# Hybrid decoder step on eight cores: the norms' transposes moved from TensorE to DMA transposes on SyncE's queue

## What is computed

```python
xn = rmsnorm(h, ln1)                              # norm 1
q, k, v, u = split(xn @ w_in)                     # 1024 -> 512 | 128 | 128 | 512
q, k = rope(q), rope(k)                           # 16 of 64 dims of each head
a  = band_attention(q, k, v, sink)                # 8 heads, 2 kv heads, window 128, learned sinks
pm = pool_mix(u, windows=(2, 4, 8, 16)) * pool_scale
h  = h + concat(a, pm) @ w_out                    # 1024 -> 1024
xn = rmsnorm(h, ln2)                              # norm 2
h  = h + relu(xn @ w_up)**2 @ w_down              # 1024 -> 4096 -> 1024
```

## Time and profile before

| | |
|---|---|
| median of 3 runs | 2930.97 us (2930.91 to 2939.81) |
| the profiled execution's own time | 2944.05 us |
| its span (slowest core, core 1) | 2942.3 us; all cores 2901.3 to 2942.3 |
| granted TensorE clock, mean | 0.979 to 0.985 of full speed |
| TensorE busy | 2779.2 us, 94% |
| VectorE, ScalarE, GpSimd busy | 1522.4, 1535.3, 195.2 us |
| DMA | 436 MB, 148 GB/s; POOL's queue 42.5%, SyncE's 9.5% of 16 engines |

### The profile page before, as it was taken

The page is one execution under the profiler, slowest core; times in us unless marked ns, Lnnn a source line. Parts: engine busy times, 40 slices in busy tenths (PEclk is TensorE's granted clock), DMA queues, the critical chain, the costliest instruction groups (busy, mean ns, idle before and its releaser), DMA issues.

```text
span 2942.3 us, 52160 instructions; the slowest of 8 cores (2901.3 to 2942.3 us)
## 1 busy us (share of the span) xinstructions
PE 2779.2 (94%) x17074; PEld 1446.1 (49%) x17074; DVE 1522.4 (52%) x3188; ACT 1535.3 (52%) x3835; POOL 195.2 (7%) x336
## 2 busy tenths in 40 slices
PE   4789988979899999999999999999899999999997
PEld 2455434445455555545455555454454545555544
DVE  2444534545355555545555555555455555555543
ACT  3545534545355555545454655555554655555543
POOL 1000100100000000000000000000000000000000
PEclk8999989999999999999999999999999999999999
DMA  9599996664756647353625332443325242342446
GB/s 177 88 145 197 178 243 122 146 169 125 195 137 161 189 113 205 101 195 123 229 87 201 114 142 93 154 132 115 117 99 188 87 167 105 117 158 87 160 145 228
DMA packets 115648, 436.41 MB, mean 148 GB/s; under 512 B 18732, under 2 KB 45324, under 8 KB 80216
## 3 DMA queue, kind: packets, MB, share of 16 engines
q0 software_dynamic: 89024, 335.80, 42.5%
q1 hardware_dynamic: 26360, 97.28, 9.5%
HBM read 442.32 MB, written 79.22 MB: 177 GB/s over the span
## 4 chain that ended last, share of the span: by engine, by line
PE 87%; DMA 9%; ACT 1%; issue 1%; DVE 1%; SPq 0%; POOL 0%; ACTq 0%; DVEq 0%; POOLq 0%
PE ps_all L1165 29%; PE ps_all L1147 29%; PE ps_all L801 10%; PE ps_all L1089 8%; DMA s_wup<-w_up 2%; PE ps_all L587 2%; PE ps_all L952 2%; PE ps_all L994 2%; DMA s_wout<-w_out 2%; DMA h_mid<-s_h 1%; DMA s_wdn<-w_dn 1%; DMA s_h<-x_p 1%; PE ps_all L954 1%; PE ps_all L953 1%; DMA s_kc<-ck 1%
## 5 line engine op out<-in xcount | busy, mean ns | idle before, releaser
L1165 PE MATMUL ps_all<-s_wdn,s_aT 128*128 128x512 bf16 x4288 | 1037.5, 382 | 21.6 <-DMA s_wdn<-w_dn 12.5
L1147 PE MATMUL ps_all<-s_xn2T,s_wup 128*128 128x512 bf16 (+2 forms) x4608 | 1023.8, 367 | 19.5 <-DMA s_wup<-w_up 13.2
L1169 DVE TENSOR_TENSOR s_h<-s_h,ps_all 128x512 f32<-128x512 f32 x1072 | 735.1, 686 | 549.1 <-PE ps_all L1165 524.7
L1147 PEld LDWEIGHTS ps_all<-s_xn2T,s_wup 128*128 128x128 bf16 x4608 | 445.1, 98 | 470.1 <-issue 31.0
L1151 ACT ACTIVATE s_relu<-ps_all 128x512 f32<-128x512 f32 (+2 forms) x576 | 326.0, 566 | 626.1 <-PE ps_all L1147 613.8
L1165 PEld LDWEIGHTS ps_all<-s_wdn,s_aT 128*128 128x128 bf16 x4288 | 406.1, 98 | 450.6 <-issue 36.1
L1152 ACT ACTIVATE s_aT<-s_relu 128x512 bf16<-128x512 f32 (+2 forms) x576 | 346.2, 601 | 39.0 <-PE ps_all L1165 5.4
L801 PE MATMUL ps_all<-s_win,s_xnT 128*128 128x512 bf16 (+1 forms) x1632 | 315.0, 350 | 22.5 <-DMA s_win<-w_in 12.6
L976 ACT ACTIVATE s_P<-ps_all,s_stat 128x256 bf16<-128x256 f32 x520 | 239.2, 476 | 91.4 <-DVE s_stat L966 91.3
L1089 PE MATMUL ps_all<-s_wout,s_mixT 128*128 128x512 bf16 x1072 | 249.8, 384 | 2.0 <-ACT s_mixT L1029 1.9
L801 PEld LDWEIGHTS ps_all<-s_win,s_xnT 128*128 128x128 bf16 x1632 | 160.7, 99 | 176.9 <-issue 36.7
(11 more groups left out here) (130 smaller groups left out, 2016.3 us busy)
## 6 DMA issues: line engine op xcount, KB each, us to landing
s_wup<-up_bf POOLq DMA_DIRECT2D x128, 1024.0 KB, 6.4
s_wdn<-dn_bf POOLq DMA_DIRECT2D x128, 1024.0 KB, 7.2
h_mid<-s_h SPq DMA_DIRECT2D x34, 512.0 KB, 8.1
s_h<-h_mid SPq DMA_DIRECT2D x34, 512.0 KB, 7.9
s_h<-x_p SPq DMA_DIRECT2D x32, 512.0 KB, 9.3
s_wup<-w_up POOLq DMA_DIRECT2D x16, 1024.0 KB, 18.0
s_wdn<-w_dn POOLq DMA_DIRECT2D x16, 1024.0 KB, 19.2
y_p<-s_h SPq DMA_DIRECT2D x32, 512.0 KB, 5.5
```

What stands on the lines that cost most here:

```text
L1147: r = e.matmul(ps_t[bk][:, 0:n], lhsT=wup_t[s][:, k, fc * 128:(fc + 1) * 128], rhs=x2[:, k, 0:n], start=(k == 0), stop=(k == 7))
L1165: r = e.matmul(ps_t[db][:], lhsT=aT[:, fc, j * 128:(j + 1) * 128], rhs=wdn_t[s][:, fc, hf * 512:(hf + 1) * 512], start=(fc == 0), stop=(fc ...
L1169: dve(lambda e, hf=hf, db=db: e.tensor_tensor(out=h_t[hs][:, hf * 512:(hf + 1) * 512], in0=h_t[hs][:, hf * 512:(hf + 1) * 512], in1=ps_t[d ...
```

## The change

From the second group on (`q` > 0), both norms leave TensorE: instead of L587, L592 and L594 one DMA transpose on SyncE's queue reads `xh` and writes `xnT`, or the tile's part of `xn2T`. No PSUM bank is taken for it. Its cost for the planner is 0.1 us of the queue and twice the 256 KB that it reads. The first group keeps its transposes on TensorE, and so do probabilities, attention outputs, q and k, and the cached keys in all groups. Where loads of x and constants waited for the first transposes on TensorE (`first_pe`), they wait for the DMA in its place if it is one.

```diff
+    def dma_T(out, in_, reads, writes, pw=(), sembuf=None):
+        def fn(e):
+            return [e.dma_start_transpose(out=out, in_=in_)]
+        return S.op("sp", fn, reads=reads, writes=writes, pwrites=pw, dma=1, sembuf=sembuf, cost=0.1, nbytes=2 * _nbytes(in_))
...
         dve(lambda e: e.scalar_tensor_tensor(out=xh[:], in0=h_t[hs][:], scalar=sT[:, 2:3], in1=g_t[gi][:], op0=ALU.mult, op1=ALU.mult),
             [h_b[hs], sB, g_b[gi]], [xhb], cost=1.29)
+        if bank is None:
+            t_op = dma_T(dstT, xh[:], [xhb], [dstT_b], sembuf=dstT_b)
+            if gi == 0:
+                first_pe.append(t_op)
+            return
         trps = ps_t[bank].bitcast(BF16)
...
-        while True:
-            bk = banks.take(1)
-            if bk:
-                break
-            yield False
-        norm_T(hs, 0, xnT, xnTb, par, bk[0])
+        by_pe = q == 0
+        if by_pe:
+            while True:
+                bk = banks.take(1)
+                if bk:
+                    break
+                yield False
+        norm_T(hs, 0, xnT[:], xnTb, par, bk[0] if by_pe else None)
         if l == 0 and ti == 0:
             load_rest()
-        banks.give(*bk)
+        if by_pe:
+            banks.give(*bk)
         yield True
...
-        norm_T(hs, 1, xn2T_t[q % 2][:, :, j * 128:(j + 1) * 128], xn2T_b[q % 2][j], par, bk[0])
-        banks.give(*bk)
+        norm_T(hs, 1, xn2T_t[q % 2][:, :, j * 128:(j + 1) * 128], xn2T_b[q % 2][j], par, bk[0] if by_pe else None)
+        if by_pe:
+            banks.give(*bk)
         yield True
```

## The result

The changed kernel takes 3140.74 us in the median of its runs (3112.67 to 3350.12) against 2935.39 for the kernel before on the same chip: a ratio of 1.0654, 95% interval 1.0559 to 1.0748. Executions in which one die ran at a lower clock, here the one of 3350.12 us, are left out of every ratio. The forecast was 2950 us, 0.6% slower, with a range up to 3080. The profiled execution has a span of 3136.4 us against 2942.3.

The account below looks back on a forecast made before the run. TensorE was taken as the bound from 800 us on, shared with the DMA engines before. Terms -59 + 22 + 27 + 15 + 14 = +19 us, on a median of 2930.97, gave 2950 us; range 2882 to 3080.

Parts of the forecast that it names:

- TensorE bounds the kernel and 0.45 us a norm comes off it: TensorE, busy 94%, bounds from 800 us on; 131 norms lose their eight transposes there, 0.45 us each: -59 us.
- Stalls and SyncE's order, 78 us together: Late landings: +22 us in layer 1, +27 from 400 to 1400 us, +15 from 100 to 400; SyncE's queue: +14.
- Evictions and PSUM banks are worth nothing; weight loads don't suffer: Evictions and banks no longer needed give nothing; weight loads on POOL's queue lose nothing from 400 us on.
- Landing about 4.8 us in layer 1, 6.1 and 8.6 before: Issue to landing of 256 KB: 4.8 us in layer 1, 6.1 from 400 to 1400 us, 8.6 from 100 to 400.
- The spread is one landing in four 2 us late: In layer 1, weight loads of 1 MB share the DMA engines: 45 exposed landings at 0.5 us, +22 us.
- 5.6 us: Landing time up to which a transpose was held to cost nothing; each microsecond beyond stalls TensorE.
- The longer chains of the two lanes, some 10 us in a group, go into the same gap, and cost 1:1 if it is used up: The gap is some 20 us of pure MLP behind the last tiles' norm-2 landings; the chains were priced at nothing.
- five exposed landings in a group: Norm 1 of tiles 1, 3, 4 and norm 2 of tiles 1, 2 are waited for; 85 in 17 groups.
- SyncE's order, +14 us: On SyncE's queue, transposes behind loads that wait for stores leave late: 0.8 us for each of 17 groups.
- named as a sign: The steps hold if TensorE's busy time falls by 59 us or more while its idle time rises by more.
- by the block, 3187 us: Rival: small pieces queue or go block by block, landings of 9.3 us or more everywhere, 315 us of stalls; chance 0.12.

Follow-up runs that it names:

- the run with the traffic alone: Kernel before, its transposes kept on TensorE, plus 130 DMA transposes of a constant on SyncE's queue that almost nothing waits for: 1.0038 of before.

## Why the prediction was wrong

- *TensorE bounds the kernel and 0.45 us a norm comes off it*: right. 54 us measured with the DMAs away, 59 forecast.
- *Stalls and SyncE's order, 78 us together*: the changed kernel is 192 us slower (1.0654 of 2935), so what was added is some 250 us, not 78. It falls into the two steps marked below.
- *Evictions and PSUM banks are worth nothing; weight loads don't suffer*: the traffic costs 0.4%, right. In the changed kernel weight pieces did come late, 45 us in 5 waits; the run with the traffic alone has none of that size, so they belong to the changed order or to its pile-ups, which I haven't taken apart.
- *Landing about 4.8 us in layer 1, 6.1 and 8.6 before*: near in layer 1 (medians 3.1 and 5.3 us, shortest 3.1), too short before it, where one of the two medians is 14.8 us both from 100 to 400 and from 800 to 1400 us. The figure of the Trainium skill for a block (VectorE: DVE Perf Modes, The three transpose paths) times eight would have been, as an estimate, 10.5 us; eight blocks in 3.1 us show that it isn't paid block by block. The statement of the Trainium skill that transposes are as fast as ordinary DMAs (Advanced Engine Details and Errata, X-Bar Transpose (TRN2)) is near for the shortest landings, 3.1 against 2.3 to 2.9 us, and doesn't hold for this kernel, where the difference is 98 us.
- *The spread is one landing in four 2 us late*: **wrong in size, the second step that failed.** 61 of 131 landings are over 5.6 us, by 405 us together where the forecast priced 64 us; they reach 37.6 us, and up to 21.7 us also where layer 1 alone has them. Single waits at the in-projection last up to 19.4 us. A fixed order pays for the tail, and a median says nothing of it.
- *"The longer chains of the two lanes, some 10 us in a group, go into the same gap, and cost 1:1 if it is used up"*: **this is the step that failed first.** I counted five exposed landings in a group, the two behind the shared xhat buffer among them, and priced only their lateness beyond 5.6 us. But the time that a punctual landing takes more than the path over PSUM lies in the lane's chain too. By the planner's costs the buffer is held 0.35 + 4.72 + 0.35 = 5.4 us in place of 0.35 + 0.45 + 0.35 = 1.15, some 4 us more. The gap didn't cover it: taking norm 2's landing out of the chain gave 3.8% (1.0654 to 1.0277) with landings that were no shorter (medians 5.8 and 6.0 us) and with nothing to gain from the buffer alone (1.0014), and making every landing due later cost 2.5% (to 1.0909). In the planner's account the change adds 73 us of TensorE idle (134 to 207) with every landing punctual, more than the 59 us that it saves; the forecast had nothing for it.
- *SyncE's order, +14 us*: not borne out. ScalarE's queue had the same landings. And of TensorE's 121 us of waits for transposes only 9 lie ahead of the issue of the one waited for, where xhat itself was late (written from 249.19 us on, its transpose issued at 250.55).
- *Not foreseen*: the clock. 37 us more of TensorE's busy time on the slowest cores, 56 on core 5, where the mean granted clock is 0.954 against 0.982. So busy time fell by 8.6 us and not by the 59 or more that was named as a sign.

The rival that came nearest in time (by the block, 3187 us) had another mechanism than what the runs show: that it is near is luck. What stays open: how the loss divides between the order and the late landings on the chip, as every run that moves the chain also moves the order; and what makes a landing of 15 to 37 us, casts in layer 0 or loads of 1 MB, which wasn't separated.

## What to carry to other kernels

Where every engine's order is fixed when the program is built, price an operation that moves to a DMA in two steps: its punctual latency in the chain of dependences, buffers that its read holds included, and its tail against the due time. Look for the write-after-read first: giving the source a buffer of its own cost two lines and took more than half of the loss. Here a later due time helped only then (4 us, 1.0%); with the chain tight it made things worse (6 us, 2.5%). Where the planner can play its orders through, compare the idle time in them before and after the change: that showed the price of the punctual landings.

## What the runs showed of the hardware

- A DMA transpose of 128x1024 bf16 inside SBUF lands 3.0 to 3.1 us after its issue at best, and holds its queue 1.2 us; a plain copy of the same bytes takes 2.3 to 2.9 us and 0.5 to 0.6. A transpose makes 1056 packets of under 512 B (157,068 against 18,732 for 131 of them), a plain copy to rows of 256 B just as many. A transpose takes 2.1 us of all 16 DMA engines, a plain copy some 0.7 (an estimate from the shares of two pages).
- 130 of them beside the kernel's own traffic cost 0.4% when nothing waits for them; 131 cost 3.3% more than plain copies when TensorE does.
- After a wait of 20.57 us eight matmuls of 512 columns took 3.53 us in place of 1.89, at a granted clock of 0.50: what the wait itself costs is not all.
